# The first norm of each stage: who adds the squares, and where their product with ones stands (hybrid mLSTM, conv and FFN layer, one core)

## What is computed

```
x = x + 0.5 * rmsnorm(swiglu(rmsnorm(x, g_ffn1_pre), w_gate, w_up, w_down), g_ffn1_post)
h = rmsnorm(x, g_mix_pre); p = h @ w_in          # queries, keys, values, gates, conv halves
x = x + rmsnorm(concat[mLSTM(p), conv(p)] @ w_out, g_mix_post)
x = x + 0.5 * rmsnorm(swiglu(rmsnorm(x, g_ffn2_pre), ...), g_ffn2_post)

rmsnorm(x, g) = x * rsqrt(mean(x * x over the 2048 features) + eps) * g
```

## Time and profile before

| | |
|---|---|
| median of 3 runs | 2172.02 us (2172.01 to 2172.33) |
| span of the profiled execution (first to last instruction) | 2170.6 us |
| the runs' median less that span | 1.4 us |
| TensorE busy | 2156.2 us, 99% |
| VectorE, ScalarE, GpSimd busy | 996.3, 902.2, 962.2 us (46%, 42%, 44%) |
| mean granted TensorE clock | 0.998 |
| DMA | 371.39 MB, mean 171 GB/s |

### The profile page before, as it was taken

The page is one execution under the profiler, slowest core; times in us unless marked ns, Lnnn a source line. Parts: engine busy times, 40 slices in busy tenths (PEclk is TensorE's granted clock), DMA queues, the critical chain, the costliest instruction groups (busy, mean ns, idle before and its releaser), DMA issues.

```text
span 2170.6 us, 41896 instructions
## 1 busy us (share of the span) xinstructions
PE 2156.2 (99%) x16326; PEld 2146.3 (99%) x16326; DVE 996.3 (46%) x1403; ACT 902.2 (42%) x1172; POOL 962.2 (44%) x561
## 2 busy tenths in 40 slices
PE   9999999999999999999999999999999999999997
PEld 9999999999999999999999999999999999999997
DVE  6533332224333225978768737643432223333323
ACT  6433333333433335634345536434343333333343
POOL 1444443344444444566656332444443334444454
PEclk9999999999999999999999999999999999999999
DMA  6454554544454544555646544544455454545453
GB/s 242 164 172 156 170 169 165 166 164 167 162 167 161 173 159 148 202 187 206 220 179 213 188 162 136 180 160 172 164 165 169 161 170 159 170 160 172 157 173 112
DMA packets 101765, 371.39 MB, mean 171 GB/s; under 512 B 11408, under 2 KB 14480, under 8 KB 100656
## 3 DMA queue, kind: packets, MB, share of 16 engines
q1 hardware_dynamic: 97488, 349.78, 48.1%
q10 hardware_dynamic: 4064, 20.33, 2.6%
q0 software_dynamic: 128, 0.07, 0.0%
HBM read 357.06 MB, written 13.07 MB: 171 GB/s over the span
## 4 chain that ended last, share of the span: by engine, by line
PE 96%; DVE 1%; ACT 1%; POOL 1%; issue 1%; DMA 0%; SPq 0%; POOLq 0%; ACTq 0%; DVEq 0%
PE bank L446 30%; PE bank L444 30%; PE bank L445 30%; PE bank L765 1%; PE bank L767 1%; PE bank L766 1%; DVE wlo L1219 0%; ACT whi L835 0%; PE bank L700 0%; POOL wlo L1737 0%; PE bank L704 0%; DMA raw<-stream 0%; PE bank L659 0%; PE bank L641 0%; DVE y L1325 0%
## 5 line engine op out<-in xcount | busy, mean ns | idle before, releaser
L1737 POOL TENSOR_TENSOR wlo<-raw,whi 128x1024 fp32r<-128x1024 f32 x332 | 798.3, 2407 | 881.5 <-ACT whi L835 762.4
L444 PE MATMUL bank<-xh,whi 128*128 128x288 f32 x3585 | 1064.4, 297 | 1.2 <-DVE xl L1240 0.9
L445 PE MATMUL bank<-xl,whi 128*128 128x288 f32 x3585 | 1059.2, 295 | 0.0
L446 PE MATMUL bank<-xh,wlo 128*128 128x288 f32 x3585 | 1057.9, 295 | 0.0
L835 ACT ACTIVATE whi<-raw 128x1024 fp32r<-128x1024 f32 x654 | 689.4, 1056 | 606.5 <-PE bank L446 576.1
L1219 DVE TENSOR_TENSOR wlo<-raw,whi 128x1024 fp32r<-128x1024 f32 x324 | 471.3, 1456 | 774.3 <-ACT whi L835 773.0
L444 PEld LDWEIGHTS bank<-xh,whi 128*128 128x128 f32 x3585 | 676.1, 189 | 4.0 <-DVE xl L1240 2.0
L446 PEld LDWEIGHTS bank<-xh,wlo 128*128 128x128 f32 x3585 | 675.0, 188 | 0.0
L445 PEld LDWEIGHTS bank<-xl,whi 128*128 128x128 f32 x3585 | 674.0, 188 | 0.4
L446 PE MATMUL bank<-hh,wlo 128*128 128x288 f32 x1408 | 417.4, 296 | 0.0
L444 PE MATMUL bank<-hh,whi 128*128 128x288 f32 x1408 | 416.1, 296 | 0.0
(11 more groups left out here) (260 smaller groups left out, 1089.4 us busy)
## 6 DMA issues: line engine op xcount, KB each, us to landing
raw<-stream SPq DMA_DIRECT2D x656, 512.0 KB, 3.4
C<-c_in ACTq DMA_DIRECT2D x4, 2048.0 KB, 8.9
cs_out<-C ACTq DMA_DIRECT2D x4, 2048.0 KB, 7.6
conv_out<-upad ACTq DMA_DIRECT2D x4, 302.0 KB, 6.5
y_out<-x_res SPq DMA_DIRECT2D x4, 288.0 KB, 2.6
upad<-conv_in ACTq DMA_DIRECT2D x4, 272.0 KB, 3.2
cp_out<-cpr ACTq DMA_DIRECT2D x4, 256.0 KB, 9.1
x_res<-x_in SPq DMA_DIRECT2D x4, 144.0 KB, 5.4
```

The lines of the kernel that those rows point to most:

```text
L444: pe.matmul(out, wh, mov_hi[:, k, :], start=first, stop=False)
L445: pe.matmul(out, wh, mov_lo[:, k, :], start=False, stop=False)
L446: return pe.matmul(out, wl, mov_hi[:, k, :], start=False, stop=last)
L1737: pool.tensor_tensor(wlo[:, g % SLOTS, :], raw[:, g % SLOTS, :], whi[:, g % SLOTS, :].bitcast(F32), ALU.subtract).then_inc(lo_ready[g % SL ...
```

## The change

VectorE's tree of four instructions is gone in all three stages. GpSimd adds instead: for c = 1 to 15 it waits for the square of chunk c and then adds `y[:, c, :]` into `y[:, 0, :]`, 128x288 at a time, each add waiting for the one before through `xsq_added`. It does so from the moment it gets there, which is during `project_first`. The last add releases `xsq_sum`. TensorE's product with ones moves from 24 matmuls behind the end of `project_first` to right behind it.

```
     # TensorE, ffn
-                        def square_sum(k):
-                            if k == 7:
-                                pe.wait_ge(xsq_sum, sums)
-                                feature_sums()
-
                         project_first(T, g, x_from)
+                        pe.wait_ge(xsq_sum, sums)
+                        feature_sums()
                         for q in range(FIRST, CH):
     # TensorE, mixer
-                if (p, j) == (MIX_FROM, CH - 1):
-                    pe.wait_ge(xsq_sum, 2)
-                    feature_sums()
+            pe.wait_ge(xsq_sum, 2)
+            feature_sums()
             for p in range(MIX_FROM, MIX):
     # VectorE, at each of the three stages (XC, 2 * XC, 3 * XC)
-            square_tree(XC)
     # GpSimd
+            def square_sum(stage):
+
+                for c in range(1, XC):
+                    pool.wait_ge(xsq_ready, XC * stage + c + 1)
+                    ins = pool.tensor_tensor(y[:, 0, :], y[:, 0, :], y[:, c, :], ALU.add)
+                    if c < XC - 1:
+                        ins.then_inc(xsq_added, 1)
+                        pool.wait_ge(xsq_added, (XC - 2) * stage + c)
+                    else:
+                        ins.then_inc(xsq_sum, 1)
     # GpSimd, ffn (and the mixer: pool.wait_ge(xsq_sum, 2) becomes square_sum(1))
-                        pool.wait_ge(xsq_sum, k + 1)
+                        square_sum(stage)
                         split_lo(g + 12)
                         split_lo(g + 13)
```

More of the change, by code:

```diff
@@ L292, in hybrid_layer_kernel @@
         sq_ready, ssq_added, ssq_clear = sem("sq_ready"), sem("ssq_added"), sem("ssq_clear")
-        xsq_ready, xsq_sum, t_ready = sem("xsq_ready"), sem("xsq_sum"), sem("t_ready")
+        xsq_ready, xsq_added, xsq_sum, t_ready = (sem("xsq_ready"), sem("xsq_added"), sem("xsq_sum"),
+                                                  sem("t_ready"))
         norm_sum, norm_sd = sem("norm_sum"), sem("norm_sd")
@@ L446, in multiply, with project @@
                 return pe.matmul(out, wl, mov_hi[:, k, :], start=False, stop=last)
-            def project(T, g, tper, gper, i, between=None):
+            def project(T, g, tper, gper, i):
                 tile_start(T, tper, i)
@@ L458, in project @@
                             last.then_inc(piece_done, 1)
-                        if between is not None:
-                            between(k)
             def project_first(T, g, x_from):
@@ L563, in ffn @@
                                 pe.wait_ge(rstd_ready, sums)
-                            project(T + q, g + 2 * q, 0, 0, None, square_sum if q == FIRST else None)
+                            project(T + q, g + 2 * q, 0, 0, None)
                         start = 2
@@ L1318, in last_residual @@
                     dve.tensor_tensor(x[:, a:b, :], t, x[:, a:b, :], ALU.add).then_inc(y_new, 1)
[L1320 to L1330, removed]
             def evict_scaled(T, tper, i, out, k=None):
@@ L1437, in _ @@
             residual(GATE_P, 0, GATE_T, "g_ffn1_post", "g_mix_pre")
-            square_tree(2 * XC)
             m0 = gv[:, 2:2 + NB].rearrange("h (b t) -> h b t", t=1)
@@ L1720, in _ @@
             residual(FFN2_P, 1, FFN2_T, "g_mix_post", "g_ffn2_pre")
-            square_tree(3 * XC)
             dve.wait_ge(cs_stored, 16 * H)
@@ L1849, in _ @@
                     pool.wait_ge(pool_chain, 4)
-            pool.wait_ge(xsq_sum, 2)
+            square_sum(1)
             split_lo(GATE_P + 12)
```

## The result

| | before | changed |
|---|---|---|
| median of 20 runs | 2172.22 us (2171.85 to 2172.72) | 2174.65 us (2174.22 to 2176.66) |
| ratio | | 1.0012, 95% interval 1.0007 to 1.0018 |
| span, first profile | 2170.6 us | 2174.9 us |
| span, second profile | 2170.3 us (e12) | 2173.2 us (e10) |
| GpSimd busy | 962.2 us | 1014.7 us |

The account below looks back on a forecast made before the run. TensorE, busy 2156.2 of 2170.6 us, bounds the kernel. Costs 0.6 + 2.2 + 0.75 = 3.55, less 0.5 gain, give +3.0: span 2173.6, median 2175.0; range of 8 in 10 2171.8 to 2180.0, own range 2173.5 to 2177.5.

Parts of the forecast that it names:

- VectorE keeps its turn: Rival: a GpSimd add starts only when VectorE leaves a hole; +1.2, 2173.2 us; chance 0.15.
- FFN 1: First stage: an add goes ahead of the x_lo of chunk 3, so TensorE stands 0.6 us longer, between 0 and 2.1.
- No harm: Rival: all adds fall beside L1298, L1301 and idle time; -0.5, 2171.5 us; chance 0.07.
- The sum is late: Rival: adds often lose their turn and xsq_sum comes behind the five tiles; +5, 2177 us; chance 0.04.
- The hold: All stages: one meeting with a GpSimd add costs a VectorE instruction with two SBUF inputs 0.6 us.
- The whole add counts: Rival: each meeting costs 0.81 us and the add ends slower; +7.9, 2179.9 us; chance 0.14.
- Mixer and FFN 2: VectorE's delay of 3.05 and 1.65 us, less 1.0 of lead, stops TensorE: 2.2 us in mixer, 0.75 in FFN 2.
- in the settled state a period loses under 0.1 us: Mixer and FFN 2: VectorE's delay shifts the squares until both adds of a period fall beside L1298 and L1301.
- 0.6 ahead of piece 9: Mixer and FFN 2: an add stands between the last x_lo and the split, delaying VectorE 0.6 us.
- The gain: Whole kernel: ended tree waits and the mixer's late GpSimd piece save 0.2 to 0.6 us, taken as 0.5.
- the two waits for the tree: TensorE's waits before the product with ones; starts 0.11 us late each, 0.2 us saved for both.
- the late piece: Mixer: a late GpSimd piece costs TensorE 0.29 us and a slow first matmul of 0.11; 0.4 saved, lower bound nothing.

Follow-up runs that it names:

- e12: The kernel before, unaltered, run as a control beside itself: 2172.07 us against 2172.08.
- e10: The changed kernel again, unaltered, for a second profile: 2174.60 us, +2.34 against the kernel before.
- e2: The changed kernel with each GpSimd add done on 8 of the 288 tokens only, leaving out most of the sum: 2171.28 us, -0.85 against before.
- e6: The changed kernel with adds placed beside VectorE's PSUM pairs (FFN 1: after chunk 9's x_lo) and the product in its old place: 2171.30 us, -0.83 against before.
- e9: The changed kernel with each GpSimd add replaced by a memset that only writes, so nothing is summed: 2171.36 us, -0.90 against before.
- e8: The changed kernel with FFN 1's adds started only when x_lo of chunk 9 is done: 2174.41 us, +2.28 against before.
- e3: The change in FFN 1 alone, mixer and FFN 2 as in the kernel before: 2172.77 us, +0.64 against before.
- e4: The change in the mixer alone, FFN 1 and FFN 2 as in the kernel before: 2173.48 us, +1.35 against before.

## Why the prediction was right

**The mechanism.** Right: GpSimd's adds and VectorE's `x_lo` and splits exclude each other, a waiting add gets in between two back-to-back VectorE instructions, and what passes VectorE's lead stops TensorE. e2, e6 and e9 show it from three sides: adds too short, in another place, or without reading. L1293 at 0.51 (changed kernel) and L1304 at 0.46 (e6), each beside an add, show that the pair on PSUM is free. "VectorE keeps its turn" falls with FFN 1: the add that asked at 11.84 went ahead of the `x_lo` issued at 12.18. "No harm" falls with the result. "The sum is late" didn't happen in the changed kernel; e8 shows how it looks when it does.

**The hold.** Forecast 0.6 us. `x_lo` are 1071 - 510 = 0.56 longer at most, splits 1.83 - 1.22 = 0.61. "The whole add counts", 0.81, falls.

**FFN 1.** 0.6 forecast, +0.64 in e3. `x_lo` of chunk 3 was held up as said. Chunk 3 started 0.54 us later behind its issue.

**Mixer and FFN 2.** The totals were about right, but partly by luck: two terms inside were wrong and cancelled. The step "in the settled state a period loses under 0.1 us" failed: it loses 0.2 (4.23 and 4.04). One add keeps meeting an `x_lo` and takes 0.40, of which 0.2 would have been idle time of VectorE anyway (e6: from 868.84 + 0.43 = 869.27 to 869.47, waiting for ScalarE). So VectorE wasn't full either, as the prediction read it: each period has this 0.2. And "0.6 ahead of piece 9" failed: the last add came just behind the start of the split, in both stages by 0.01 us, and waited. In rows of the changed kernel, FFN 2, GpSimd and VectorE:

```profile
1349.83 1.88 POOL L1731 TENSOR_TENSOR y<-y 128x288 f32<-128x288 f32 x1 [1.31 <-ACT y L870]
1349.82 4.11 DVE L1214 TENSOR_TENSOR wlo<-raw,whi 128x1024 fp32r<-128x1024 f32 x3
```

So the delay in FFN 2, 0.9 us at the first split, grew by 0.2 in each of the four periods behind it, to 1.7, and not at the end. The stop was at piece 8, 0.77 + 0.11 for the restart = 0.88, where 0.75 was forecast. In the mixer the stops at pieces 5 to 8 add up to 1.9 to 2.0 us with their restarts, where 2.2 was forecast: 0.11 + 0.08 at piece 5, 0.10 + 0.11 at 6, 0.40 + 0.11 at 7, 0.95 + 0.11 at 8. (In single-stage kernels the gains are in the difference too: +1.35 and +0.78.)

**The gain.** Mis-sized: 0.2 to 0.6 us, taken 0.5; e2, e6 and e9 have 0.83 to 0.90 without the loss. The term that was too small is the two waits for the tree. The prediction took for each only the 0.11 by which the product starts late. But the product's two matmuls take 0.75 behind the wait and 0.65 without it (e6, TensorE):

```profile
885.28 0.65 PE L514 MATMUL bank<-y,ones 128*128 128x288 f32 x2
```

So one wait costs 0.11 + 0.10 = 0.21 and two 0.42, where 0.2 was taken, and the late piece costs 0.29 + 0.11 = 0.40 as was said. That is 0.82, about the whole gain. Matmul by matmul, e6 gains 0.20 us on before at 885 us, 0.41 at 898 and 0.23 at 1353, and under 0.1 anywhere else behind FFN 1; the changed kernel gains the same three.

What ends the late piece is not the earlier root that the prediction named first. In e6 the root starts as in before (885.96 and 886.07), and the late piece is gone all the same. VectorE's reciprocal comes earlier, because before had a meeting of its own there: a GpSimd split, released by the tree, started 0.03 us ahead of VectorE's L1445, a `tensor_tensor` of only 128x4 on SBUF. It takes 2.37 us; in e6 the same instruction comes at 881.54 and takes 0.14. The reciprocal stands right behind it. So the prediction's other reason, gate work behind the tree, is right, but most of that work's length was the meeting. GpSimd and VectorE before, then VectorE in e6:

```profile
885.31 7.12 POOL L1737 TENSOR_TENSOR wlo<-raw,whi 128x1024 fp32r<-128x1024 f32 x3 [28.99 <-DVE y L1325]
885.34 2.37 DVE L1445 TENSOR_TENSOR pick<-ident 128x4 fp32r<-128x4 f32 x1
887.64 1.93 DVE L1225 RECIPROCAL rstd<-scr 128x288 f32<-128x288 f32 x1
```
```profile
886.50 1.95 DVE L1228 RECIPROCAL rstd<-scr 128x288 f32<-128x288 f32 x1 [4.81 <-ACT scr L847]
```

The earlier product of the changed kernel adds nothing: its root starts at 885.96, too.

**What had no term.** The meeting of L1524 with a GpSimd split at 902, and the stop of 0.57 us that it brings. L1524 takes 2.6 to 3.1 us in four of the six profiles with the mixer's product right behind the five tiles (the first of the changed kernel, e2, e8, e9; not e4, e10) and 1.08 or 1.09 in all seven with the old place. It stops TensorE for more than 0.1 us only in the first profile and in e8's. So the median hardly holds it.

**The sum.** Loss 3.55 forecast, 3.3 measured (2.43 + 0.85), and 0.6 + 1.95 + 0.88 = 3.4 by the stops; gain 0.5 and 0.85; +3.0 and +2.43. The forecast's own range, 2173.5 to 2177.5, holds the time.

## What to carry to other kernels

Work taken off an engine that doesn't bound the kernel is worth only the waits it ends, here 0.85 us for 15.7 us of VectorE time, and about half of that was a meeting of before that the new order avoids. What it does beside that engine in its new place can cost more: look for what both read from SBUF, count the meetings, and compare the delay with the lead over the engine that binds. If GpSimd must read SBUF beside a VectorE with little lead, let each of its instructions wait for the start of one of VectorE's that reads PSUM; here the semaphores that were already there were enough. Where VectorE's lead has grown, as in FFN 1 from chunk 9 on, the reads can meet it at no cost. And count what a wait costs behind its end too: here 0.1 us each time.

## What the runs showed of the hardware

- GpSimd's add of 128x288 is listed with 0.81 us and holds up a VectorE instruction with two SBUF inputs for 0.56 to 0.61 us; a memset of 128x576, 0.58 us, doesn't hold it up at all (541 ns for `x_lo` at most, 510 in the median).
- A GpSimd split of 128x1024 (2.4 us) holds up even a tiny VectorE `tensor_tensor` on SBUF that is issued just behind it: 3.13 us instead of 1.09 for 4x896, 2.37 instead of 0.14 for 128x4.
- An add that asks while VectorE is busy goes next, though VectorE's following instruction stands right behind (asked at 11.84 under a split, ahead of the `x_lo` at 12.18). One that asks 0.01 us behind VectorE's start waits for all of it (1349.83, 1.88 us instead of 0.81).
- An instruction of VectorE with one of its two inputs in PSUM isn't held up by an add: 0.51 (L1293) and 0.46 us (L1304 in e6).
- A wait of TensorE costs about 0.11 us more than itself: the first matmul behind it is listed with 0.40 instead of 0.29, and the next starts 0.11 later. Behind the waits for the tree the product's two matmuls take 0.75 instead of 0.65.
- In one of two profiles of the same kernel the granted clock fell to 0.50 for 3 us at 908 us, 1.5 us of time; ahead of it TensorE had stood for 0.57 us. A stop of 0.52 us at the same place in e8's profile had no such stretch behind it.
